# An expert layer's weight loads in another order, and its last sum ahead of the next layer's weight split

## The reference, cut to what matters

```python
# first_block: 16 experts, each token goes to 2 of them
y = moe_ffn(tokens, w_router, b_router, w_exp_gate, w_exp_up, w_exp_down)
x = x + gt2 * y                       # expert_block: (silu(xb @ w_g[e]) * (xb @ w_u[e])) @ w_d[e]
x = rms_norm(x, g_final)
# second_block, for each of 2 layers:
h = rmsnorm(x, norm_mix[l]) @ w_in[l] # and many products more
mk, mv = jnp.split(rmsnorm(mem, norm_mem[l]) @ w_mem_kv[l], 2, axis=-1)   # needs no x
```

## Time and profile before

| what | value |
|---|---|
| median of three runs | 2625.09 us |
| the profiled execution: its time, its span | 2625.09 us, 2623.3 us |
| TensorE busy | 2507.7 us, 96% |
| VectorE busy | 1282.7 us, 49% |
| ScalarE busy | 1018.1 us, 39% |
| bytes moved, mean rate | 602.49 MB, 230 GB/s |
| block 0 starts, block 15 ends on TensorE | 441.94 us, 1135.73 us |

### The profile page before, as it was taken

How to read it: one execution, slowest core, us unless ns; L and a number is a source line. 1 busy time by engine, 2 the same in 40 slices (tenths; PEclk the granted TensorE clock), 3 DMA queues, 4 the chain that set the end, 5 groups by cost and what they waited for, 6 DMA issues and landing times. The chain is left out here.

```text
span 2623.3 us, 39235 instructions
## 1 busy us (share of the span) xinstructions
PE 2507.7 (96%) x15703; PEld 1825.5 (70%) x15703; DVE 1282.7 (49%) x1857; ACT 1018.1 (39%) x1264; POOL 180.9 (7%) x210
## 2 busy tenths in 40 slices
PE   5999999999999999989999999999999999999998
PEld 3756786433333333368897888899898978888996
DVE  3444674121212121145687575655456786756453
ACT  4433552221212121234556453444345555534432
POOL 0000010000000000000083000000000650000000
PEclk9999999999999999999999999999999999999999
DMA  7343657999999999974343035444543440254452
GB/s 292 146 175 143 235 185 306 421 421 393 420 421 420 420 421 420 420 275 161 129 161 129 34 127 199 178 178 165 204 169 135 155 161 34 102 204 176 165 189 96
DMA packets 78944, 602.49 MB, mean 230 GB/s; under 512 B 15956, under 2 KB 21652, under 8 KB 24664
## 3 DMA queue, kind: packets, MB, share of 16 engines
q1 hardware_dynamic: 78808, 600.53, 58.6%
HBM read 599.45 MB, written 1.05 MB: 229 GB/s over the span
## 5 line engine op out<-in xcount | busy, mean ns | idle before, releaser
L2158 DVE TENSOR_TENSOR weight_slabs_rounded<-weight_slabs,arena_rounded 128x2048 fp32r<-128x2048 f32 x206 | 475.0, 2314 | 354.1 <-ACT arena_rounded L2155 315.6
L2155 ACT ACTIVATE arena_rounded<-weight_slabs 128x2048 fp32r<-128x2048 f32 x206 | 392.7, 1914 | 357.3 <-PE psum_vector L555 226.2
L553 PE MATMUL psum_scalar<-arena_rounded,arena_rounded 128*128 128x256 f32 (+1 forms) x1456 | 472.3, 324 | 21.4 <-DVE weight_slabs_rounded L2158 9.8
L553 PE MATMUL psum_vector<-arena_rounded,arena_rounded 128*128 128x512 f32 (+3 forms) x1264 | 455.4, 360 | 13.1 <-issue 6.7
L555 PE MATMUL psum_vector<-arena_rounded,arena_rounded 128*128 128x512 f32 (+1 forms) x896 | 348.6, 389 | 0.0
L554 PE MATMUL psum_vector<-weight_slabs_rounded,arena_rounded 128*128 128x512 f32 x880 | 343.9, 391 | 0.0
L1953 DVE TENSOR_TENSOR arena<-psum_scalar,arena 64x512 f32<-64x512 f32 x96 | 65.5, 683 | 541.6 <-ACT arena L1883 537.0
L553 PEld LDWEIGHTS psum_scalar<-arena_rounded,arena_rounded 128*128 128x128 f32 x1456 | 279.6, 192 | 53.9 <-issue 24.7
L554 PE MATMUL psum_scalar<-arena_rounded,arena_rounded 128*128 128x256 f32 x992 | 281.9, 284 | 0.0
L555 PE MATMUL psum_scalar<-arena_rounded,weight_slabs_rounded 128*128 128x256 f32 x992 | 281.9, 284 | 0.0
L553 PEld LDWEIGHTS psum_vector<-arena_rounded,arena_rounded 128*128 128x128 f32 (+2 forms) x1264 | 238.0, 188 | 52.7 <-issue 18.3
(11 more groups left out here) (490 smaller groups left out, 3204.3 us busy)
## 6 DMA issues: line engine op xcount, KB each, us to landing
weight_slabs<-in_layer_slabs SPq DMA_DIRECT2D x100, 2048.0 KB, 7.7
arena<-in_expert_slabs SPq DMA_DIRECT2D x192, 1024.0 KB, 20.2
weight_slabs<-in_expert_slabs SPq DMA_DIRECT2D x96, 1024.0 KB, 21.8
weight_slabs<-in_mixer_slabs SPq DMA_DIRECT2D x32, 2048.0 KB, 8.2
weight_slabs<-in_layer_slabs SPq DMA_DIRECT2D x6, 1024.0 KB, 5.4
arena<-in_b_gate SPq DMA_DIRECT2D x6, 512.0 KB, 8.4
arena<-in_mem SPq DMA_DIRECT2D x2, 1024.0 KB, 11.7
arena<-in_x SPq DMA_DIRECT2D x1, 1024.0 KB, 5.0
```

Source lines behind the costliest of these rows:

```text
L553: pe.matmul(out, left[0], right[0], start=start, stop=False)
L2155: e.activation(fr(high), low, ACT.Copy).then_inc(S("weights_high"), 1)
L2158: e.tensor_tensor(fr(low), low, fr(high).bitcast(F32), ALU.subtract).then_inc(S("weights_split"), 1)
```

## The change

It has two parts. In `sp_moe` both loops take their order from one function. The first loop now covers i = 0 to 11 and has the order of the old first loop. The second covers i = 12 to 14 and differs from the first only behind half 17: 9, 7, 8, 10 to 15 in place of 9 to 15, 7, 8. At the end of `vec_moe` the product with the gate and the sum into x stand ahead of the split of half slab 0, and the split of half slab 1 stands behind the scaling of x.

```diff
@@ sp_moe
-            with sp.Fori(0, 4) as i:
+            def block(i, *behind):
+
                 this, following = expert_of(i), expert_of(i + 1)
                 halves_of(following, i + 1, *range(7))
                 halves_of(this, i + 1, 16, 17)
-                halves_of(following, i + 1, *range(9, 16), 7, 8)
-            with sp.Fori(4, last_) as i:
-                this, following = expert_of(i), expert_of(i + 1)
-                halves_of(this, i + 1, 16, 17)
-                halves_of(following, i + 1, *range(16))
+                halves_of(following, i + 1, *behind)
+
+            with sp.Fori(0, 12) as i:
+                block(i, *range(9, 16), 7, 8)
+            with sp.Fori(12, last_) as i:
+                block(i, 9, 7, 8, *range(10, 16))
             halves_of(expert_of(last_), last_ + 1, 16, 17)
@@ vec_moe
             step = Count(e, S("vector_between"))
+            e.wait_ge(m["vector_full"], MOE_V * last_ + MOE_V + 1)
+            step(tt(yacc, psv[:].rearrange("p (t b) n -> p t (b n)", b=2), over(gt2, NT), ALU.mult))
+            step(tt(x, x, yacc, ALU.add))
+            e.sem_inc(S("x_expert"), 1)
             first_layer = Splitter(e, 0, high=False)
             first_layer.upto(0)
-            e.wait_ge(m["vector_full"], MOE_V * last_ + MOE_V + 1)
-            step(tt(yacc, psv[:].rearrange("p (t b) n -> p t (b n)", b=2), over(gt2, NT), ALU.mult))
-            first_layer.upto(1)
-            step(tt(x, x, yacc, ALU.add))
-            e.sem_inc(S("x_expert"), 1)
             e.wait_ge(S("squares"), ROOTS_SO_FAR)
...
             step.sync()
             e.sem_inc(S("x_ready"), 1)
+            first_layer.upto(1)
             return step
```

## The result

The kernel after takes 2641.87 us in the median of 6 runs (2637.42 to 2647.32), the kernel before 2626.4 us on the same chip (2620.81 to 2630.04). The ratio is 1.0061, with a 95% interval of 1.0045 to 1.0077: slower by 15.5 us. The prediction was 2636.0 us, 2628 to 2641; the direction came as forecast, the median lies 0.9 us above the range. The profiled execution took 2643.13 us with a span of 2641.3.

What follows compares the result with a forecast made beforehand. The experts were taken as bound by the weight stream at 420 GB/s, the rest not. Block 15's start 7.1, halves 7 and 8 0.5, clock 2.9 and passage 0.4 put 10.9 us on 2625.1: 2636.0 us, range 2628 to 2641.

Steps and rivals of the forecast that it cites:

- Where block 15 starts: End of the experts: block 15 starts at 1104.2 us instead of 1090.32, ends at 1142.8 against 1135.73: +7.1 us.
- The price of the dry queue: Change from first to second loop, block 4: the DMA queue ran dry before; 2.9 us won back, already in +7.1.
- Halves 7 and 8, and the clock: Late expert blocks: +0.5 us for halves 7 and 8 waiting on reads, +2.9 us for lumped waits lowering the clock.
- Rival (a): Blocks 13 and 14: the clock stays up, giving 2633.1 us; chance 0.2.
- The passage: Experts to layer 0: PE starts later, but no wait before the third half slab; +0.4 us, bounds -4.0 and +4.1.
- Rival (b): Experts to layer 0: the new VectorE order pays, -2.7 in place of +0.4 us, 2633 or 2630 us; chance 0.2.
- The sum: Whole kernel: 7.1 + 0.5 + 2.9 + 0.4 = 10.9 us, added to 2625.1 us, gives 2636.0 us.
- The upper end of the range: Whole kernel: 2641 us, from the upper bounds of the clock and of halves 7 and 8.

Runs made afterwards that it cites:

- The three doses: Kernel after with one, four or seven halves of the following block ahead of 16 and 17 in iterations 12 to 14: 692.1, 695.4, 703.5 us from block 0's start to block 15's end.
- the part alone: Kernel before with only the new SyncE transfer order, VectorE as before: 2633.62 us against 2625.8, ratio 1.0030.
- The three kernels with one half ahead: Kernel after with one half ahead (2626.94 us); also with split, product, sum, split at the passage (2623.57); that plus three idle products behind the last combine (2627.2).
- The three traces of after: Kernel after, unedited, in its first timing and two repeats: 2641.87, 2638.22 and 2639.5 us.
- the other order: Kernel after with the first loop's order in iterations 12 to 14 too, halves 7 and 8 last: 2637.57 us against 2625.79, ratio 1.0048.
- the third trace: Kernel after, unedited, run a third time: 2639.5 us against 2625.26, ratio 1.0047.
- four halves ahead: Kernel after with four halves of the following block ahead of 16 and 17 in iterations 12 to 14: 2629.5 us against 2625.26, ratio 1.0018.
- The second trace of before: Kernel before, unedited, timed against itself: 2624.23 us against 2625.26, ratio 0.9989.
- Part 2 alone: Kernel before with only the new VectorE order at the passage, SyncE as before: 2627.18 us against 2625.8, ratio 1.0007.

## Why the prediction was right in its cause and short in its size

**Where block 15 starts: right.** Forecast +13.9 us for its start at a full queue, -6.8 for its length, +7.1 together. Measured: block 4 begins at b0 + 168.20 (before 168.51), blocks 4 to 12 take 44.88 each, block 15 takes 38.56 without a wait for a transfer. What is over in blocks 13 and 14 (45.60 and 47.26, 3.1 above two periods of 44.88) is the next term. The three doses show the mechanism, and the part alone shows that nothing else carries it. The price of the dry queue didn't enter this sum, since block 15's start was counted at a full queue; it was probably put low. The three kernels with one half ahead (692.08, 691.93 and 693.56 us up to E) gain 0.9 us in the mean over before although their queue loses 2.8 in blocks 12 and 13, which makes it 3.7, and the rate in block 4 gives 42.92 x (1 - 378/420) = 4.3, where the prediction took 2.9.

**Halves 7 and 8, and the clock: right within the bounds.** Forecast 0.5 + 2.9. The three traces of after have 92.86, 92.81 and 92.38 us for blocks 13 and 14, where the other order has 89.77: 2.9 us in the mean. The division was off, and that the sum came out is partly luck. In iteration 12 the queue didn't run dry: halves 7 and 8 land 2.5 us behind the transfer in front, each. In iteration 13, behind the first low clock, they land 3.8 and 3.3 us behind it, 2.2 us lost where the prediction had 0.5 and 1.2 for the two causes. In this trace half 16 of block 14 then comes after 4.82 us of idleness, not 3.4. Block 13 is longer than the period by 0.72 us, since it had time to spare, block 14 by 2.38, of which 5.27 x 0.32 = 1.7 is the clock. That split isn't fixed either: in the third trace block 13 is longer by 1.9 and block 14 by 0.8. Together from b0 to E: 703.5 - 693.4 = 10.1, forecast 10.5. Rival (a), a clock that stays up, is out: it fell behind such a wait in all three traces of after, in the part alone and with one wait of 3.36 us at four halves ahead. The Trainium skill, "TensorE: Matmul & The Clock Gate", section "Loop structure matters more than you think", warned of long waits for DMA between matmuls. The traces agree: sixteen matmuls in 5.35 us behind the one wait, where sixteen take 3.65 behind the short ones.

**The passage: the places right, the size not.** The prediction had +0.4 us for it. PE starts at E + 11.64 (forecast 11.5), the third half slab at E + 24.51 (24.8), no wait before it. In these two traces the term is 39.64 - 39.40 = +0.2. But before's low clock behind the wait of 2.28 us, which I entered as a fixed 1.7, isn't fixed. The second trace of before waits 2.05 us at this place, in PE's timeline, and keeps its clock, in the stretch behind it:

```profile
1163.61 0.39 PE L553 MATMUL psum_scalar<-arena_rounded,arena_rounded 128*128 128x256 f32 x1 [2.05 <-DVE weight_slabs_rounded L2158]
```

```profile
1163.61:1178.83 15.22, 15.22 (x129) 15.22 (x130) 9.86 (x13) 8.16 (x8) 0.70 (x1) 1.00 0.69 215
```

There the fifth half slab comes at E + 37.93. And behind after's 7.20 us the clock is low for 2.94 us here, but for longer in its third trace (E + 40.93). Means of three and of two traces: 40.1 - 38.7 = **+1.4**, in place of +0.4. Part 2 alone has 39.73, 1.1 above before's mean. This is the mis-sized term of the sum. Rival (b), a passage that pays, is refuted by the same numbers.

**The sum.** Over the touched part after needs 743.6 us (743.25, 743.00, 744.55) and before 732.0 (733.18, 730.89): +11.6, forecast +10.9. The timings gave +15.5, +12.4 and +14.2, of which up to 1 is the comparison's own. So 3.9, 0.8 and 2.6 us of them lie outside the touched part. The traces don't hold them: from the fifth half slab to the end they have 1450.28, 1449.45 and 1447.28 us in after and 1448.18 and 1448.03 in before, and b0 lies at 445.0 us in the mean of after and at 444.9 in that of before. But each timed run also has its mean granted clock. Multiplied out as (1 - clock) x span, the low clock is 25 to 27 us in the mean of the runs of before, in three comparisons of 26 to 35 runs. In after it is 36.6, 32.0 and 34.7 us in 8, 7 and 6 runs, in the order of the three timings. That is 6.6 to 11 us more, and the low stretches in the touched part of the traces make up 5.4 of it. The rest, about 1 to 5 us, is low clock elsewhere, and it is largest where the time is. The other kernels of this study have 26 to 30 us. Why the whole change should have more low clock in places that it doesn't touch stays open, and the three timings of after differ by 3 us among themselves.

**The step that failed** is the adding up. The sum ended at the third half slab and was put on 2625.1 us, the time of one profiled run. So it had the low clock of the rest of the kernel at nothing, without a reason, and at the passage as the same 1.7 us on both sides. In its place the runs showed +1.4 us for the passage and +0.8 to +3.9 us outside the touched part, on a kernel before whose median is 2626.4: together 2626.4 + 11.6 + 3.9, the 2641.9 measured. The upper end of the range has the same fault. It adds the upper bounds of two terms to the 2625.1 and stops at 2641, while the spread of the runs widens only the lower end.

## What to carry to other kernels

In a kernel bound by its weight stream, as this one, count what is still to be transferred behind the last piece of the last block but one: if that takes less time than the whole last block, every transfer put ahead of that piece lengthens the kernel by its own time, however full the queue is. An order that is right in the steady state has to be given back towards the end of the stream, and there in small doses (here one half ahead, not seven). At a change of stage, put into an engine's wait what needs only old data, and no more: one split ahead of the sum hides, both sum and product ahead of the split don't.

## What was not expected of the hardware

- At the same wait the clock isn't the same in each execution: before the third half slab 2.05 us kept 1.00, and 2.28 us were followed by a stretch at 0.64 in the mean. All 24 waits of 2.98 us and more that the traces of this study have between b0 and the fifth half slab were followed by a low clock; its length differed between traces of the same program.
- Identical instructions ahead of block 0 took 441.5 to 447.9 us; the two traces of before, at 441.9 and 447.9, have 0.97 and 0.95 as mean granted clock. The Trainium skill, "TensorE: Matmul & The Clock Gate", section "What's actually happening", has the number of slow matmuls at the start of one kernel vary from run to run. In these two traces it isn't the start: the first 60 us have 0.91 in both, and the difference lies from 60 to 300 us (0.99 and 0.97) and from 415 us up to b0 (0.81 and 0.74). 6 us out of 2626 is more than most edits of this study moved.
- Waits of 0.6 to 1.3 us spread over a block cost nothing but themselves; the same time in one wait cost 2.9 us more in two blocks, by a dry queue and the clock. Block 15 gives 2.4 us of it back, since its halves 7 and 8 are then in time.
